# A squared-ReLU feed-forward in two phases, its second product made of seven block products in place of eight

## The chip, the cores and the metric

The kernel runs on one core of a Trainium2 chip. Its time is the device time of one execution in microseconds (us), lower is better; the median of several runs counts. The engines named below are TensorE (PE, matrix products), VectorE (DVE), ScalarE (ACT), GpSimd (POOL) and SyncE (SP, which here only issues transfers between DRAM and the on-chip memory).

## The reference

One layer of a conditioned decoder trunk on x of 2048 tokens by 1024 channels, in float32. The part that the change touches is the squared-ReLU feed-forward; the token mixer before it (attention, convolutions, pooling and the output projection `w_out`) stays, but its last stage for the second half of the tokens borders on it.

```python
x = x + g1 * mix                                   # mix = concatenate([...]) @ w_out[l]
h = rms_norm(x, norm2_g[l]) * (1.0 + sc2) + sh2
x = x + g2 * (jnp.square(jax.nn.relu(h @ w_ff1[l])) @ w_ff2[l])
# w_ff1: 1024 x 4096, w_ff2: 4096 x 1024
```

## The kernel before

Tokens are worked on in two halves (`hc` = 0, 1) of 1024. For each half the output projection runs first (`out_part`, 8 rows of 128 tokens, each with two column blocks of 512), then the feed-forward. Between them x is normalised and turned into `h_hi` and `h_lo`.

A float32 product is made of three products of rounded operands. Each operand is split into a high part (ScalarE copies it into the type float32r: a "head") and the rest (VectorE subtracts: a "tail"), and TensorE adds hi x hi, hi x lo and lo x hi. Every matmul of the feed-forward has 128 stationary columns and 512 moving ones.

The hidden width of 4096 is cut into 16 groups `g` of 256. Per group:

- The first product gives u = relu(w1ᵀ h)² for 256 hidden rows and 1024 tokens. The two first groups (`plain`) do it directly with 96 matmuls. The other 14 (`fast`) use seven block products in place of eight (Winograd's form), 84 matmuls; they need three combinations of h made once per half (`comb_add`, `comb_tail`, `difference_tail`, `last_comb_sum`) and four sums of the group's weights (`w1_sum1` to `w1_sum4`), and their seven results go through PSUM banks 0 to 3 with copies by ScalarE (`seeded`, `copied`, `reseeded`).
- The second product (`second`) follows at once, direct: 16 output tiles (8 token tiles, two column blocks of 512) of 6 matmuls each, 96 a group, in PSUM banks 4 to 7. VectorE adds each tile to `x_new`, the half's x in on-chip memory (`accumulate`). The gate g2 has been multiplied into the weights of w_ff2 (`w2_fold`), then they are split.

Each engine has its own order, written out by hand, and semaphores tie them together. SyncE issues all loads, each when its buffer comes free. Groups 3 to 15 run in hardware loops (`Fori`). Rows of the result are stored from `x_new` as the last group's tiles are added.

## Time and profile before

| | |
|---|---|
| median of 3 runs | 2357.76 us (2356.51 to 2361.86) |
| span of the profiled execution, first to last instruction | 2354.6 us |
| TensorE busy | 2283.8 us, 97% |
| VectorE busy | 1746.0 us, 74% |
| ScalarE busy | 971.2 us, 41% |
| DMA, mean over the span | 75 GB/s |

The profile comes from one execution. Its span begins with the first and ends with the last instruction. What that execution took around its span is not recorded; the three timed runs lie 1.9 to 7.3 us above the span. Matmuls overlap, so the duration of one (389 ns) is longer than the distance from one start to the next; the second is what a stage costs. VectorE's short operations overlap a little too.

### The profile page before, as it was taken

What the parts mean: (1) busy time and instruction counts of PE and PEld (TensorE: products, weight loads), DVE (VectorE), ACT (ScalarE), POOL (GpSimd) and SP (SyncE); (2) the same over time, 40 slices, a digit from 0 to 9 for tenths busy, and PEclk for the clock granted to TensorE, in tenths of its full rate; (3) what the DMA queues carried; (4) which work ended last, traced back from release to release, by engine and by line L of the source; (5) the groups of instructions that cost most, each with busy time, mean ns of one, the idle gap of its engine ahead of it and who ended that gap; (6) DMA issues with size and microseconds to landing.
All of it is one profiled execution on the core that took longest, in us unless ns stands there. A gap on an engine that the chain in (4) does not pass through costs nothing.

```text
span 2354.6 us, 31383 instructions
## 1 busy us (share of the span) xinstructions
PE 2283.8 (97%) x11642; PEld 1924.3 (82%) x11642; DVE 1746.0 (74%) x2659; ACT 971.2 (41%) x1595; POOL 357.9 (15%) x285
## 2 busy tenths in 40 slices
PE   6999999988999999999999999999999999999999
PEld 5987898767889888888888888888888888888887
DVE  6648886889989876876767767676787676767676
ACT  4531555458888844332323232233432323222231
POOL 0442044824356610000000000000000000000000
PEclk9999999989999999999999999999999999999999
DMA  7441533120000152011111111145111111111112
GB/s 270 155 152 63 157 129 118 63 89 28 15 10 24 52 155 81 18 54 54 53 53 53 37 61 45 54 132 189 63 36 53 54 36 62 45 53 53 53 53 89
DMA packets 108280, 177.68 MB, mean 75 GB/s; under 512 B 5512, under 2 KB 77468, under 8 KB 107164
## 3 DMA queue, kind: packets, MB, share of 16 engines
q1 hardware_dynamic: 108100, 176.41, 22.6%
q8 instruction: 58, 0.95, 0.2%
q14 instruction: 34, 0.28, 0.0%
q10 hardware_dynamic: 88, 0.04, 0.0%
HBM read 152.84 MB, written 23.59 MB: 75 GB/s over the span
## 4 chain that ended last, share of the span: by engine, by line
PE 81%; DVE 10%; DMA 3%; issue 2%; ACT 2%; POOL 2%; SPq 0%; ACTq 0%; DVEq 0%; POOLq 0%
PE ps L2513 10%; PE ps L2512 10%; PE ps L2511 10%; PE ps L2550 8%; PE ps L2548 8%; PE ps L2549 8%; PE ps L2210 5%; PE ps L2212 5%; PE ps L2211 5%; PE ps L2401 3%; DVE ps L1615 2%; PE ps L2458 2%; PE ps L2456 2%; PE ps L2457 2%; DMA sb_w_raw<-in_w_in 2%
## 5 line engine op out<-in xcount | busy, mean ns | idle before, releaser
L1997 DVE TENSOR_TENSOR sb_x_new<-sb_x_new,ps 128x512 f32<-128x512 f32 x512 | 347.2, 684 | 107.5 <-PE ps L2513 102.0
L2511 PE MATMUL ps<-sb_w_hi,sb_u_hi 128*128 128x512 f32 x1024 | 398.3, 389 | 0.0
L2512 PE MATMUL ps<-sb_w_lo,sb_u_hi 128*128 128x512 f32 x1024 | 398.3, 389 | 0.0
L2513 PE MATMUL ps<-sb_w_hi,sb_u_lo 128*128 128x512 f32 x1024 | 398.3, 389 | 0.0
L2512 PEld LDWEIGHTS ps<-sb_w_lo,sb_u_hi 128*128 128x128 f32 x1024 | 192.2, 188 | 39.9
L2511 PEld LDWEIGHTS ps<-sb_w_hi,sb_u_hi 128*128 128x128 f32 x1024 | 192.2, 188 | 39.9
L2513 PEld LDWEIGHTS ps<-sb_w_hi,sb_u_lo 128*128 128x128 f32 x1024 | 192.2, 188 | 39.9
L2212 PE MATMUL ps<-sb_h_hi,sb_w_lo 128*128 128x512 f32 x512 | 199.4, 389 | 0.0
L1428 ACT ACTIVATE ps<-ps 128x512 f32<-128x512 f32 x28 | 16.3, 582 | 410.8 <-PE ps L2550 410.8
L2210 PE MATMUL ps<-sb_h_hi,sb_w_hi 128*128 128x512 f32 x448 | 177.5, 396 | 0.7 <-DVE sb_w_lo L1958 0.7
L2211 PE MATMUL ps<-sb_h_lo,sb_w_hi 128*128 128x512 f32 x448 | 174.4, 389 | 0.0
L2548 PE MATMUL ps<-sb_h_hi,sb_ring_hi 128*128 128x512 f32 x448 | 174.3, 389 | 0.0
L2549 PE MATMUL ps<-sb_h_lo,sb_ring_hi 128*128 128x512 f32 x448 | 174.3, 389 | 0.0
L1354 ACT ACTIVATE sb_u_hi<-sb_u_full 128x512 fp32r<-128x512 f32 x128 | 81.0, 632 | 192.0 <-DVE sb_u_full L1986 114.2
L1837 DVE TENSOR_SCALAR_CACHE_REDUCE sb_scores<-ps 128x1024 f32<-128x1024 f32 (+7 forms) x160 | 139.5, 891 | 12.4 <-PE ps L2424 6.9
L2401 PE MATMUL ps<-sb_v_sb,sb_a_t 128*128 128x64 f32 x1088 | 140.7, 270 | 0.0
L1615 DVE SCALAR_TENSOR_TENSOR ps<-sb_conf,sb_col,ps 128x512 f32<-128x512 f32 x208 | 140.4, 747 | 0.0
L2401 PEld LDWEIGHTS ps<-sb_v_sb,sb_a_t 128*128 128x128 f32 x1088 | 136.4, 195 | 0.5 <-ACT sb_q_stack L1258 0.2
L2421 PE MATMUL ps<-sb_k_stack,sb_q_stack 128*128 128x512 f32 (+3 forms) x320 | 112.8, 417 | 23.2 <-DVE sb_scores L1837 18.3
L2550 PE MATMUL ps<-sb_h_hi,sb_w_lo 128*128 128x512 f32 x336 | 130.7, 389 | 0.0
L2548 PE MATMUL ps<-sb_w_hi,sb_ring_hi 128*128 128x512 f32 x336 | 130.7, 389 | 0.0
L2549 PE MATMUL ps<-sb_w_lo,sb_ring_hi 128*128 128x512 f32 x336 | 130.7, 389 | 0.0
(291 smaller groups left out, 4947.9 us busy)
## 6 DMA issues: line engine op xcount, KB each, us to landing
sb_w_full<-in_w_ff SPq DMA_DIRECT2D x34, 1024.0 KB, 4.9
sb_w_full<-in_w_ff SPq DMA_DIRECT2D x56, 512.0 KB, 3.7
sb_w_raw<-in_w_in SPq DMA_DIRECT2D x16, 1024.0 KB, 5.6
sb_ada<-in_w_ada SPq DMA_DIRECT2D x32, 512.0 KB, 5.0
sb_ada_first<-in_w_ada SPq DMA_DIRECT2D x8, 1024.0 KB, 13.7
sb_x_in<-in_x SPq DMA_DIRECT2D x16, 512.0 KB, 5.4
sb_mix_in<-mix_scratch SPq DMA_DIRECT2D x16, 512.0 KB, 4.9
sb_x_new<-in_x SPq DMA_DIRECT2D x16, 512.0 KB, 4.9
```

The lines of the kernel that those rows point to most:

```text
L1615: ins = V.scalar_tensor_tensor(out=dst, in0=src, scalar=w, in1=dst, op0=ALU.mult, op1=ALU.add)
L1997: V.tensor_tensor(out=y, in0=y, in1=psum[:, 4 + p % 4, :], op=ALU.add).then_inc(ff2_read, 1)
L2210: M(dst, ah, bh, start=(n == 0), stop=False)
L2211: M(dst, ah, bl, start=False, stop=False)
L2212: ins = M(dst, al, bh, start=False, stop=(n == last))
L2401: ins = M(psum[:, 6 + i % 2, hd * VD:(hd + 1) * VD], a_t[gn % 3][:, k * P:(k + 1) * P], v_sb[:, k0 + k, hd * VD:(hd + 1) * VD], start=(k0 ...
L2511: M(dst, uh, wh[:, j, col], start=j == order[0], stop=False, skip_group_check=fast)
L2512: M(dst, uh, wl[:, j, col], start=False, stop=False, skip_group_check=fast)
L2513: ins = M(dst, ul, wh[:, j, col], start=False, stop=j == order[1], skip_group_check=fast)
L2548: M(psum[:, bank, :], wh[:, k, :], rh[:, k, :], start=fresh and k == 0, stop=False, skip_group_check=True)
L2549: M(psum[:, bank, :], wh[:, k, :], rl[:, k, :], start=False, stop=False, skip_group_check=True)
L2550: ins = M(psum[:, bank, :], wl[:, k, :], rh[:, k, :], start=False, stop=k == DC // 2 - 1, skip_group_check=True)
```

## The change

The feed-forward of a half is split into two phases.

- Phase one makes the first products of all 16 groups and no second product. Each u (four blocks: two of hidden rows by two of tokens) is not split, but stored to DRAM in the seven forms that the second phase needs: three blocks of u as they are and four sums (`u_sums`, `u_sum4`), 256 KB each, into `left_scratch`.
- Phase two works through 8 chunks `c` of 512 hidden rows. Each chunk is a product of 1024 tokens x 512 by 512 x 1024, made of seven block products ("slots") of 512 x 256 by 256 x 512 in place of eight. SyncE loads the seven left blocks (512 KB each) and the right side (2 MB of w_ff2); VectorE makes four sums of the right side (`right_add`); both sides of each slot are split (`heads`, `left_tail`, `right_tail`). All eight PSUM banks hold results: side 0 is banks 0 to 3, side 1 is banks 4 to 7. ScalarE copies between the sides (`seed_lower`, `seed_upper`), and VectorE reads five partial results per chunk, each in two pieces of two banks, into sums in on-chip memory (`evacuate`).
- Since x no longer fits beside these, it goes to DRAM after the output projection (`x_mid_scratch`) and comes back in the last chunk. There the gate g2 is multiplied onto the results, by GpSimd for the upper rows (`finish_upper`) and VectorE for the lower, and x is added.
- The weights of phase one are double-buffered by group, with one 1 MB load each; the loops are written out.
- The two plain groups now follow each other directly, and the output projection of the second half follows the last chunk of the first.

The core of the diff, cut ("..." marks what is left out). TensorE:

```diff
-                def second(g, p, js, fast):
-                    t, cb = tile_no(p, fast)
-                    wh, wl = by_k2(w_hi[3][:, :]), by_k2(w_lo[3][:, :])
...
                 def plain(g):
...
                         if f >= 2:
                             pe.wait_ge(relu_ready, 4 * (PLAIN * hc + g) + f - 1)
+                        elif g and f == 0:
+                            pe.wait_ge(relu_ready, 4 * (PLAIN * hc + g))
...
                 def fast(g):
                     n = FAST * hc - PLAIN + g
-                    fast_product(n, 0, 0, True, rows(0, 0))
-                    if g is PLAIN:
-                        pe.wait_ge(t_lo, 4 * hc + 3)
-                    fast_product(n, 1, 2, True, combined(0)[0:2])
+                    if g == PLAIN:
+                        pe.wait_ge(relu_ready, 4 * PLAIN * (hc + 1))
+                    else:
+                        pe.wait_ge(fast_relu, 2 * n - 1)
+                    fast_product(g, 0, 0, True, slot(0)[0:2])
...
+                def multiply(G, s, t, side, fresh):
+
+                    hi, low, _ = slot(s)
+                    dst, tok = psum[:, 4 * side + t, :], slice(t * P, (t + 1) * P)
+                    for k in range(2):
+                        M(dst, hi[:, k, tok], hi[:, 2 + k, :], start=fresh and k == 0, stop=False, skip_group_check=True)
+                        M(dst, hi[:, k, tok], low[:, 2 + k, :], start=False, stop=False, skip_group_check=True)
+                        ins = M(dst, low[:, k, tok], hi[:, 2 + k, :], start=False, stop=k == 1, skip_group_check=True)
+                    ins.then_inc(part_mm, 1)
+
+                def chunk(c):
+                    G, last = chunk_no(hc, c), c == CHUNKS - 1
+                    for s in order_of(c):
+                        pe.wait_ge(slot_lo, 2 * (SLOTS * G + s) + 2)
+                        for t in range(4):
+                            if s == 0 and c:
+                                pe.wait_ge(part_read, read_no(hc, c - 1, 5, t // 2))
...
+                            elif s == 1:
+                                pe.wait_ge(part_copied, copy_no(G, 0, t))
+                            elif s == 3:
+                                pe.wait_ge(part_copied, copy_no(G, 1, t))
+                            elif s == 5:
+                                pe.wait_ge(part_read, read_no(hc, c, 1 if last else 3, t // 2))
+                            elif s == 6:
+                                pe.wait_ge(part_read, read_no(hc, c, 4, t // 2))
+                            multiply(G, s, t, 1 if s in (2, 4, 6) else 0, s in (0, 5))
```

`order_of(c)` is 0 to 6, and 0, 1, 5, 2, 3, 4, 6 in the last chunk of a half. ScalarE, the end of the plain groups and phase two:

```diff
+                relu(1, 1)
+                w1_head(PLAIN, 0)
+                w1_head(PLAIN, 1)
+                w1_head(PLAIN, 2)
+                relu(1, 2)
+                w1_head(PLAIN, 3)
+                w1_head(PLAIN, 4)
+                w1_head(PLAIN, 5)
+                w1_head(PLAIN, 6)
+                relu(1, 3)
+                last_comb_head()
...
+                def seed_upper(c):
+                    G = chunk_no(hc, c)
+                    for t in range(4):
+                        act.wait_ge(part_mm, part_no(G, order_of(c).index(2), t))
+                        act.wait_ge(part_read, read_no(hc, c, 5 if c == CHUNKS - 1 else 1, t // 2))
+                        A(psum[:, t, :], psum[:, 4 + t, :], ACT.Copy).then_inc(part_copied, 1)
+
+                for c in range(CHUNKS - 1):
+                    heads(c, 5)
+                    seed_lower(c)
+                    heads(c, 6)
+                    heads(c + 1, 0)
+                    seed_upper(c)
+                    for s in range(1, 5):
+                        heads(c + 1, s)
```

VectorE, the second plain group, a fast group, and phase two:

```diff
-                def accumulate(g, p, fast=False):
-                    t, cb = tile_no(p, fast)
-                    y = x_new[:, t, cb * BLK:(cb + 1) * BLK]
-                    dve.wait_ge(ff2_mm, 16 * g + (16 * FG * hc + p + 1))
-                    V.tensor_tensor(out=y, in0=y, in1=psum[:, 4 + p % 4, :], op=ALU.add).then_inc(ff2_read, 1)
...
+                link(comb_add(t1, b22[0], t2, ALU.subtract))
+                comb_add(t1, t1, b22[1], ALU.add).then_inc(t_summed, 1)
+                u_sums(0)
+                u_sum4(0)
+                difference_tail()
+                last_comb_sum()
+                plain_square(1, 0)
+                comb_tail(1, 2)
+                plain_square(1, 1)
+                comb_tail(0, 3)
+                w1_sums(PLAIN)
+                for i in range(3):
+                    w1_tail(PLAIN, i)
+                plain_square(1, 2)
...
+                        dve.wait_ge(fast_relu, 2 * n)
+                        square(1, 0)
+                        u_sum4(g - 1)
+                    if last:
+                        right_add(0, 0)
+                        right_add(0, 1)
+                    else:
+                        w1_sums(g + 1)
+                        for i in range(3):
+                            w1_tail(g + 1, i)
                     dve.wait_ge(fast_relu, 2 * n + 1)
                     square(0, 0)
-                    dve.wait_ge(fast_mm, 7 * n + 5)
+                    if last:
+                        tails(0, 0)
...
+                for c in range(CHUNKS - 1):
+                    if c:
+                        evacuate(c - 1, 6, 1)
+                        tails(c, 5)
+                    else:
+                        tails(0, 2)
+                        dve.wait_ge(fast_relu, 2 * (fast_no(FG - 1) + 1))
+                        square(1, 0)
+                        u_sum4(FG - 1)
+                        tails(0, 3)
+                        tails(0, 4)
+                        tails(0, 5)
+                    tails(c, 6)
+                    right_add(c + 1, 0)
+                    evacuate(c, 1, 0)
+                    evacuate(c, 1, 1)
...
+                if hc == 0:
+                    wo_tail(1, 1)
+                    mix_tail(HT)
+                    mix_tail(HT + 1)
+                for t in range(4):
+                    dve.wait_ge(part_mm, part_no(chunk_no(hc, c), SLOTS - 1, t))
+                    ins = V.tensor_tensor(out=out21[:, t, :], in0=psum[:, 4 + t, :], in1=gate_row[:, 1, 0:BLK], op=ALU.mult)
```

SyncE, a fast group and phase two:

```diff
+                        fast_done(hc, g - 1, SLOTS)
+                    if g < FG - 1:
+                        load_w1(hc, g + 1)
+                    else:
+                        load_right(0)
+                    store_left_sums(hc, g - 1)
+                    if g > PLAIN:
+                        store_left_u(hc, g - 1, 5, 4)
+                    store_left_sum4(hc, g - 1)
...
+                for ch in range(CHUNKS - 1):
+                    G = chunk_no(hc, ch)
+                    if ch == 0:
+                        sp.wait_ge(slot_lo, 2 * SLOTS * G + 8)
+                        sp.wait_ge(right_summed, 4 * G + 4)
+                        load_right(1)
+                    for s in range(SLOTS):
+                        if s == 6 and ch + 2 < CHUNKS:
+                            sp.wait_ge(slot_lo, 2 * SLOTS * (G + 1) + 8)
+                            sp.wait_ge(right_summed, 4 * (G + 1) + 4)
+                            load_right(ch + 2)
+                        sp.wait_ge(part_mm, part_no(G, s, 3))
+                        load_left(hc, ch + 1, s)
```

## Rows read from the trace of the kernel before

**Rows 1.** The page, its first part: busy time and share of the span by engine.

```profile
PE 2283.8 (97%) x11642; PEld 1924.3 (82%) x11642; DVE 1746.0 (74%) x2659; ACT 971.2 (41%) x1595; POOL 357.9 (15%) x285
```

**Rows 2.** Window: busy PE, PEld, DVE, ACT, POOL; clock, DMA share, GB/s.

```profile
1000.00:1650.00 650.00, 650.00 (x2885) 538.58 (x2884) 457.08 (x625) 188.49 (x287) 0.00 (x0) 1.00 0.22 71
```

**Rows 3.** Waits: who waited for whom, us in total, times, longest.

```profile
ACT ps L1428 <- PE ps L2550: 410.8, 28, 15.2
...
DVE sb_x_new L1997 <- PE ps L2513: 102.0, 154, 0.7
```

**Rows 4.** Timeline, PE, border of the halves: start, us, engine, line.

```profile
1556.26 0.39 PE L2548 MATMUL ps<-sb_h_hi,sb_ring_hi 128*128 128x512 f32 x1
...
1575.30 0.39 PE L2511 MATMUL ps<-sb_w_hi,sb_u_hi 128*128 128x512 f32 x1
...
1597.06 0.39 PE L2456 MATMUL ps<-sb_w_hi,sb_h_hi 128*128 128x512 f32 x1
```

**Rows 5.** Groups by form, from 1000 us: busy us, mean ns, idle before.

```profile
L1997 DVE TENSOR_TENSOR sb_x_new<-sb_x_new,ps 128x512 f32<-128x512 f32 x496 | 337.1, 684 | 107.4 <-PE ps L2513 102.0
...
L1380 ACT ACTIVATE sb_ring_hi<-sb_w_full 128x512 fp32r<-128x512 f32 x112 | 69.7, 622 | 1.3
...
L1434 ACT ACTIVATE ps<-ps 128x512 f32<-128x512 f32 x28 | 16.3, 582 | 44.9 <-PE ps L2550 44.9
...
L1284 ACT ACTIVATE sb_h_hi<-sb_mix_in 128x1024 fp32r<-128x1024 f32 x8 | 8.4, 1047 | 0.2 <-DMA sb_mix_in<-mix_scratch 0.2
```

**Rows 6.** Timeline, DVE: operations of 512, then of 1024 and 2048 columns.

```profile
1544.47 0.68 DVE L1997 TENSOR_TENSOR sb_x_new<-sb_x_new,ps 128x512 f32<-128x512 f32 x1
1545.07 0.68 DVE L2026 TENSOR_TENSOR sb_w_lo<-sb_w_full,sb_ring_hi 128x512 fp32r<-128x512 f32 x1
...
1594.45 1.22 DVE L1873 TENSOR_TENSOR sb_h_lo<-sb_mix_in,sb_h_hi 128x1024 fp32r<-128x1024 f32 x1
1595.59 1.28 DVE L1997 TENSOR_TENSOR sb_x_new<-sb_x_new,ps 128x512 f32<-128x512 f32 x2
...
1599.27 2.29 DVE L1894 TENSOR_TENSOR sb_w_lo<-sb_wo_raw,sb_w_hi 128x2048 fp32r<-128x2048 f32 x1
```

**Rows 7.** DMA issues: count, KB each, median us from issue to landing.

```profile
sb_w_full<-in_w_ff SPq DMA_DIRECT2D x34, 1024.0 KB, 4.9
sb_w_full<-in_w_ff SPq DMA_DIRECT2D x56, 512.0 KB, 3.7
...
sb_ada_first<-in_w_ada SPq DMA_DIRECT2D x8, 1024.0 KB, 13.7
...
sb_v_sb<-qkv_scratch SPq DMA_DIRECT2D x1, 2048.0 KB, 10.0
```

**Rows 8.** Last tail of h, second half; TensorE's feed-forward began at 1691.0.

```profile
L2210 PE MATMUL ps<-sb_h_hi,sb_w_hi x32: 389/389/504, 1691.0 to 1713.6; 128*128 128x512 f32 x32
...
1701.88 1.23 DVE L1493 TENSOR_TENSOR sb_h_lo<-sb_h_tmp,sb_h_hi 128x1024 fp32r<-128x1024 f32 x1 [0.40 <-ACT sb_h_hi L1018]
```

**Rows 9.** Groups of POOL: its commonest operation of 1024 columns.

```profile
L908 POOL TENSOR_TENSOR sb_gate_row<-sb_gate_row,sb_ada 128x1024 f32<-128x1024 f32 x21 | 52.9, 2532 | 55.7 <-ACT sb_ada L1139 55.7
```

**Rows 10.** Timeline of the end; the span is 2354.6 us.

```profile
2350.49 0.39 PE L2513 MATMUL ps<-sb_w_hi,sb_u_lo 128*128 128x512 f32 x1
2350.91 0.69 DVE L1997 TENSOR_TENSOR sb_x_new<-sb_x_new,ps 128x512 f32<-128x512 f32 x1 [0.67 <-PE ps L2513]
```

**Rows 11.** Timeline of PE around a gap in the attention stage.

```profile
824.48 0.61 PE L2386 MATMUL ps<-sb_ident,sb_scores 128*128 128x128 f32 x4
...
825.76 0.61 PE L2386 MATMUL ps<-sb_ident,sb_scores 128*128 128x128 f32 x4
...
830.68 1.11 PE L2386 MATMUL ps<-sb_ident,sb_scores 128*128 128x128 f32 x4 [2.02 <-ACT sb_a_t L1258]
...
833.19 1.06 PE L2386 MATMUL ps<-sb_ident,sb_scores 128*128 128x128 f32 x4
```

**Rows 12.** Window behind that gap: the columns are those of rows 2.

```profile
831.00:833.00 2.00, 2.00 (x12) 2.00 (x11) 2.00 (x2) 0.72 (x2) 0.82 (x1) 0.50 1.06 402
```

More of the change, by code:

```diff
@@ L837, in _ @@
+                for e in range(HT):
+                    store_out(hc, e)
+                    if hc == 0 and e == HT // 2 - 1:
+                        load_rows(1, 0)
+                        load_rows(1, 1)
+            for p in range(HT // 2):
+                sp.wait_ge(out_st[p], 64)
         @block.gpsimd
@@ new lines, in fast @@
+                    if last:
+                        heads(0, 1)
+                        heads(0, 2)
+                        heads(0, 3)
+                    else:
+                        for i in range(3, SLOTS):
+                            w1_head(g + 1, i)
+                    act.wait_ge(fast_mm, SLOTS * n + 7)
+                    last_square_free(g)
+                    A(u_full[1][0][:, :], psum[:, 1, :], ACT.Relu).then_inc(fast_relu, 1)
+                for g in range(PLAIN, FG):
+                    fast(g)
@@ L1453, in _ @@
+                heads(CHUNKS - 1, 5)
+                seed_lower(CHUNKS - 1)
+                heads(CHUNKS - 1, 6)
+                seed_upper(CHUNKS - 1)
                 if hc == 0:
-                    for i in range(3):
-                        wo_head(1, i)
+                    G = chunk_no(0, CHUNKS - 1)
+                    wo_head(1, 0, (part_mm, part_no(G, 1, 3)))
+                    wo_head(1, 1, (part_mm, part_no(G, 3, 3)))
+                    act.wait_ge(part_mm, part_no(G, 4, 3))
@@ L2155, in fast @@
                     square_of_positive(1, 1)
-                    u_tail(g, 1, 0, 0)
-                    u_tail(g, 2, 1, 1)
-                    dve.wait_ge(fast_mm, 7 * n + 6)
+                    if last:
+                        right_add(0, 2)
+                        right_add(0, 3)
+                    else:
+                        for i in range(5, SLOTS):
+                            w1_tail(g + 1, i)
+                    dve.wait_ge(fast_mm, SLOTS * n + 6)
                     V.tensor_tensor(out=u_full[0][1][:, :], in0=psum[:, 3, :], in1=u_part[:, :],
@@ L2189, in _ @@
-                with dve.Fori(PLAIN + 1, FG - 1) as g:
-                    fast(g)
-                fast(FG - 1, last=True)
-                for p in range(4, 16):
-                    if hc == 0 and p in (6, 8, 10):
-                        wo_tail(1, p // 2 - 3)
-                    if hc == 0 and p in (12, 14):
-                        mix_tail(HT + p // 2 - 6)
-                    accumulate(FG - 1, p, True)
-                if hc == 0:
+                    if last:
+                        tails(0, 1)
@@ L2587, in _ @@
                 for g in range(PLAIN):
                     plain(g)
-                fast(PLAIN)
-                with pe.Fori(PLAIN + 1, FG) as g:
+                for g in range(PLAIN, FG):
                     fast(g)
+                for c in range(CHUNKS):
+                    chunk(c)
 INPUTS = ["x", "c", "w_ada", "b_ada", "norm1_g", "norm2_g", "w_in", "w_out", "q_norm_g", "k_norm_g",
```

878 lines of the change are left out of this document (506 added, 372 removed).

## The prediction, written before the changed kernel was run

> **What bounds the kernel now.** I read the totals of the page first, then the windows, the waits and the timelines of the feed-forward. TensorE is busy for 97% of the span and VectorE for 74% [rows 1]. The windows say where the rest lies: from 1000 to 1650 us, over the border of the halves, TensorE is busy for all 650 us at full granted clock [rows 2]. The chain of waits agrees: VectorE and ScalarE wait there for TensorE, not TensorE for them [rows 3]. A busy TensorE is not yet TensorE at its pace, so I take the pace from the timeline: a group's first product starts at 1556.26, its second at 1575.30 and the next stage at 1597.06 [rows 4]. That is 84 matmuls in 19.04 us and 96 in 21.76 us, both 0.2267 us each, without a gap over the border of a half. So the feed-forward costs its number of matmuls times 0.2267 us; a matmul that goes away is worth that, as long as nothing else falls due first.
>
> **What is removed.** Before, the second product of a half is 16 groups of 96 matmuls, 1536. Now it is 8 chunks of 7 block products of 4 token tiles, 2 hidden blocks and 3 part products: 8 x 7 x 24 = 1344. Over two halves 384 go: 384 x 0.2267 = **87.0 us**. The first product keeps its matmuls, and the shape (128 columns stationary, 512 moving) stays.
>
> **Phase one, one fast group (84 matmuls, 19.04 us).** VectorE loses its 16 accumulations, the fold of the gate and the splits of u; it keeps 4 weight sums, 7 weight tails, 4 squares, 2 sums, and gains 4 sums of u: 21 operations of 512 columns. Each is listed at about 0.69 us [rows 5], but ready ones follow each other after 0.60 us [rows 6]: 12.6 us by pace, 14.5 us by duration. ScalarE has 5 reads of PSUM and 7 heads of 0.62 us, 7.3 us [rows 5]. The order matters more. The next group's weights (1 MB, one issue) are only asked for when the previous group ends, and land 4.9 us later [rows 7]; with issue at about 5.3 us. From there VectorE runs 4 sums (7.8), 3 tails (10.6), a square after the fourth product (12.1), 2 tails (13.3), the sum that frees bank 1 (14.3), a square, 2 tails, the second sum (17.0), a square and 3 sums of u (19.7), while its next work, the last square, falls due at 19.8. TensorE needs bank 1 for its seventh product at 16.3, so 2 us are spare. I cost the 28 groups at nothing; the cover is that spare time. The seven stores of 256 KB per group and the load are 2.8 MB; two rows that differ by 512 KB differ by 1.2 us [rows 7], so about 7 us of transfer in 19. The removed loops give nothing back, since the groups already follow without a gap [rows 4].
>
> **Phase two, one chunk (168 matmuls, 38.08 us).** VectorE has 14 tails, 4 sums of the right side and 10 evacuations, all of 1024 columns. No row shows an evacuation of two banks at once; at 512 columns a read from PSUM costs the same 0.684 us as one from SBUF [rows 5], so 1.15 us by pace [rows 6], 1.22 by duration: 28 x 1.15 = 32.2 us, at most 34.2. ScalarE: 14 x 1.05 + 8 x 0.58 = 19.3 us. Both are under 38.08. In the program's order the tightest date is the copy of side 1 to side 0 before the fourth product (16.3 us into the chunk): it needs the evacuation of the second product (due 8.2, done 9.4) and a ScalarE that has got past the heads for the next chunk's slot 0. The 2 MB of the right side are asked for some 5 us before the chunk starts. The nearest rows are 4.9 us for 1 MB plus 2.5 for a second one, 7.4, and 10.0 for a 2 MB load [rows 7]; so they are there at 3 to 5 us, and the date holds with over 5 us spare. Steady chunks: nothing.
>
> **The plain stage of each half.** The second products of the two plain groups, 43.5 us of cover, are no longer between the first ones. TensorE needs 2 x 21.76 us, but VectorE must in that time form and split the combinations of h and prepare seven weights. Counted from TensorE's start, its last tail of h ends at 12.1 [rows 8]. Following the program at 0.6, 1.15 and 2.2 us for 512, 1024 and 2048 columns (2.29 listed [rows 6], less the overlap): first pass over the combinations 14.4, square 15.0, second pass 17.2, tail of the second weights 19.4, two squares, a wait for the fourth relu, 23.8 (TensorE waits too, 0.8 us, since the second plain group now needs all four), square, two passes 28.9, four sums of u 31.6, tail 33.9, fourth combination 38.7, two squares and two tails 44.3, first weight sum 44.9, fourth 46.9. ScalarE has three heads behind those sums ahead of the last relu, and four more: that relu ends at 49.7. TensorE would be done at 45.6 and its next product waits for that relu: 4.1 us. Together 5.0 us a half, **10.0 us** (0 to 20: three microseconds of VectorE either way count in full).
>
> **From phase one to two.** In the last group the 2 MB load comes first and the u stores behind it. I put the right side at 9 us (7.4 to 12), the first left block at 11. ScalarE does the heads of slot 0 ahead of the relu of bank 0, so that ends at 13.6; VectorE's square and two tails follow, and the sum that frees bank 1 ends at 17.2 against 16.3: 0.9 us. TensorE enters chunk 0 at 20.0. VectorE is behind: tails of slot 2 at 28.4, of slot 3 at 32.0, only then may the next 2 MB be asked for, landing at 40. VectorE's sum of that right side stands *before* the evacuation of the second product. So the evacuation due at 31 ends at 42.4, the copy at 43.6, and TensorE, which was ready at 36.3, starts its fourth product at 43.7: 7.4 us. Per half 8.3 us, **16.7 us** (6 to 28).
>
> **Between the halves.** Before, there is no gap [rows 4]. Now the output projection waits until VectorE has read the last block's first two tiles, and that stands behind scaling, adding, a weight tail of 2.2 us and two mix tails: read at 43.7 of the last chunk, which TensorE leaves at 38.5. Then the weight tails of parts 2 and 3 cost 0.6, and the last product began 0.4 late: **6.3 us** (3 to 12). GpSimd's finish of the upper rows, 2.5 us each of eight steps [rows 9], lies beside this.
>
> **The end.** Today the last matmul starts at 2350.49, VectorE ends at 2351.6, the span at 2354.6 [rows 10]: 3.7 us after the last matmul. Afterwards VectorE owes two scalings and two additions more and is a little behind: about 7.1 us, so **3.4 us**.
>
> **The clock.** After a gap of 2.02 us a round of 12 small matmuls takes 2.5 us in place of 1.3 [rows 11], and the granted clock is 0.50, which is 1.2 GHz [rows 12]; two such rounds cost 2.4 us. The three gaps above 6 us would each bring this: **7.2 us** (0 to 12; the two of 4 us might as well). The Trainium skill (TensorE: Matmul & The Clock Gate, Why this matters for your kernels) says that TensorE sent waiting between bursts of matmuls falls back to half its clock; this case's trace agrees, with its 0.50. By that rule the change loses at five places; without any such loss the sum would give 2307.
>
> **Sum.** -87.0 + 10.0 + 16.7 + 6.3 + 3.4 + 7.2 = -43.4. The profiled span of 2354.6 becomes 2311.2. The runs lie 3.2 us above the span (median 2357.76), so 2314.4; I say **2314 us**.
>
> **Rivals.**
> A (0.12): the borders are covered after all. For it: VectorE's dates there hang on landings that I put late. Half of my stalls and no clock loss leave 18 us: 2289.
> B (0.20): phase one is paced by VectorE behind the weight load. For it: 2 us are all that is spare, and with other traffic a 1 MB load took up to 13.7 us [rows 7]. Against: here it stands ahead of the stores. If it lands at 8.5 us, each group loses 1.2 us, 28 groups 34: 2348.
> C (0.05), the other side: the same load lands above 9 us. From 7.3 us on every microsecond is paid 28 times; the remaining 43 us of gain are gone at 1.5 us per group, so from 8.8 us on the kernel is slower; at 9.5 it is 2.2 us per group, 62 us: 2376.
> D (0.05): a chunk is paced by VectorE. At 1.4 us an operation a chunk takes 39.2, 16 x 1.1 = 18 us: 2332. The widest 1024-column row, 1.22, speaks against it.
> The forecast has the remaining 0.58.
>
> **How the numbers follow.** The forecast's own range, from the bounds above, is 2295 to 2335. The 80% range reaches halfway into A and into the mild end of B: 2292 to 2345. No change means within 0.2%, 4.7 us, which a measurement of this kernel can just tell. Slower is C, 0.05; same, between B and C, 0.03; faster 0.92.
>
> **What the profile afterwards would show.** 1344 matmuls a half in the second product, at 0.2267 us; fast groups 19.04 us apart and chunks 38.1; gaps of TensorE of about 4 us before the first fast group, 7 before chunk 0's fourth product, 5 between the halves, each followed by a granted clock of 0.50. I am wrong if fast groups are over 19.3 us apart (B, C), chunks over 38.3 (D), or the borders are closed (A).

## The result, and the profile after

The changed kernel takes 2344.09 us (median of 4 runs, 2341.91 to 2347.80), the kernel before 2359.64 us on the same chip: a ratio of 0.9937 (95% interval 0.9922 to 0.9951), 15.6 us faster. A second comparison of the same pair on another occasion gave 2343.36 against 2356.66 us, 0.9950 (0.9937 to 0.9964). So the change is worth some 13 to 16 us; the forecast was a gain of 43, and 2344 us lies at the very end of the range (2292 to 2345) and outside the forecast's own (2295 to 2335). The direction was right, two thirds of the gain are missing.

The page of the changed kernel, its head and first part:

```profile
span 2346.0 us, 29756 instructions
...
PE 2230.1 (95%) x11258; PEld 1875.4 (80%) x11258; DVE 1840.0 (78%) x2575; ACT 1121.7 (48%) x1787; POOL 404.3 (17%) x301
```

TensorE has exactly 384 matmuls fewer than in [rows 1], and VectorE is busy for 94 us more. The profiled execution is the slowest of the four (2347.8 us), and the profiled one of before, with its span of 2354.6, was the fastest of its four (2356.51). So the two spans differ by 8.6 us only, where the medians differ by 15.6. I account for these 8.6.

Windows of the changed kernel, columns as in [rows 2]: up to the feed-forward, its first half, the output projection of the second half, the second feed-forward, and a stretch inside the first half (each row ends with the granted clock, the share of the transfers and GB/s):

```profile
0.00:943.60 943.60, 881.48 (x5378) 765.83 (x5378) 738.32 (x1315) 555.18 (x965) 358.06 (x285) 0.97 0.30 100
943.60:1596.30 652.70, 626.16 (x2721) 514.88 (x2721) 520.40 (x583) 269.91 (x378) 23.78 (x8) 0.98 0.46 159
1596.30:1692.50 96.20, 95.86 (x440) 79.38 (x440) 64.75 (x96) 35.87 (x76) 0.00 (x0) 0.98 0.39 131
1692.50:2338.40 645.90, 626.16 (x2719) 515.31 (x2720) 512.82 (x579) 260.75 (x372) 22.50 (x8) 0.98 0.45 153
1000.00:1250.00 250.00, 250.00 (x1105) 207.07 (x1104) 176.60 (x275) 87.97 (x157) 0.00 (x0) 1.00 0.47 155
```

From 1000 to 1250 us TensorE is busy throughout at full granted clock, as before: the fast groups run as forecast. But each half of the feed-forward has about 20 to 26 us in which TensorE does nothing, and the mean clock of a half is 0.98 in place of 1.00. The timeline of TensorE shows where; these are the first matmuls behind its waits (start, duration, line, and in brackets the idle time and who ended it):

```profile
993.37 0.75 PE L2844 MATMUL ps<-sb_h_hi,sb_w_hi 128*128 128x512 f32 x1 [3.49 <-ACT sb_u_full L1590]
...
1264.71 0.79 PE L2844 MATMUL ps<-sb_h_hi,sb_w_hi 128*128 128x512 f32 x1 [5.62 <-DVE sb_u_full L2375]
1265.30 0.63 PE L2845 MATMUL ps<-sb_h_lo,sb_w_hi 128*128 128x512 f32 x1
1265.73 0.63 PE L2846 MATMUL ps<-sb_h_hi,sb_w_lo 128*128 128x512 f32 x1
...
1291.00 0.77 PE L2878 MATMUL ps<-sb_h_hi 128*128 128x512 f32 x1 [4.52 <-ACT ps L1677]
...
1579.18 0.47 PE L2878 MATMUL ps<-sb_h_hi 128*128 128x512 f32 x1 [3.63 <-DVE sb_out L2343]
...
1587.94 0.80 PE L2878 MATMUL ps<-sb_h_hi 128*128 128x512 f32 x1 [4.44 <-DVE sb_out L2343]
...
1596.29 0.76 PE L2772 MATMUL ps<-sb_w_hi,sb_h_hi 128*128 128x512 f32 x1 [4.02 <-DVE sb_out L2508]
...
2333.63 0.79 PE L2878 MATMUL ps<-sb_h_hi 128*128 128x512 f32 x1 [4.89 <-DVE sb_out L2343]
```

The first half has six such gaps, the second four, of 3.6, 5.1, 5.6 and, in its last chunk, 5.1 us. Behind each of them the matmuls start 0.43 us apart (1265.30 to 1265.73), not 0.2267; the window 1264.70 to 1269.50 has a granted clock of 0.50. From gaps (start to start, less 0.23) and from the slow matmuls (their distance less 0.2267) comes the ledger, in us of the profiled span:

| term | forecast | measured, half 0 + half 1 |
|---|---|---|
| 384 matmuls | -87.0 | -87.0 (pace 0.2267) |
| plain stage | +10.0 | +9.2 (4.6 + 4.6) |
| phase one to two, chunk 0 | +16.7 | +21.2 (10.5 + 10.7) |
| last chunk, and between the halves | +6.3 | +17.9 (12.8 + 5.1) |
| end (last matmul to the end of the span) | +3.4 | +3.5 |
| clock behind the gaps | +7.2 | +19.6 (10.4 + 9.2) |
| before the feed-forward starts | 0 | +6.3 |
| sum | -43.4 | -9.3 (span: -8.6) |

The row "before the feed-forward starts" is not the change: the instructions there are the same. The feed-forward starts at 937.29 us in the trace of before and at 943.61 in this one, and in the twelve traces of experiments below, whose work up to there is the same too, anywhere from 936.25 to 943.60, with a median of 940.1. It differs by stretches of low clock in the attention stage: from 700 to 800 and from 800 to 900 us the granted clock is 0.97 and 0.93 in the first trace of the changed kernel, and 1.00 in both in the run that starts at 936.25. One trace of before, of its fastest execution, can't say whether a shift of one to three microseconds is left in the mean.

### The profile page after: what moved, and what is told of

Read it like the earlier page. It is cut to its first block and busy times, and to the rows that moved or that the text cites. A ratio compares the mean times of both kernels' runs of the same rounds, so it can differ in the third digit from the quotient of the medians.

```text
span 2346.0 us, 29756 instructions
## 1 busy us (share of the span) xinstructions
PE 2230.1 (95%) x11258; PEld 1875.4 (80%) x11258; DVE 1840.0 (78%) x2575; ACT 1121.7 (48%) x1787; POOL 404.3 (17%) x301
## 5 line engine op out<-in xcount | busy, mean ns | idle before, releaser
L2878 PE MATMUL ps<-sb_h_hi 128*128 128x512 f32 x512 | 203.6, 398 | 23.1 <-DVE sb_out L2343 13.0
L2879 PE MATMUL ps<-sb_h_lo,sb_h_hi 128*128 128x512 f32 x512 | 202.2, 395 | 0.0
L2880 PE MATMUL ps<-sb_h_hi,sb_h_lo 128*128 128x512 f32 x512 | 202.2, 395 | 0.0
L2844 PE MATMUL ps<-sb_h_hi,sb_w_hi 128*128 128x512 f32 x448 | 178.2, 398 | 17.6 <-DVE sb_u_full L2375 10.6
L2527 PE MATMUL ps<-sb_h_hi,sb_w_hi 128*128 128x512 f32 x448 | 177.8, 397 | 0.7 <-DVE sb_w_lo L2195 0.7
L2845 PE MATMUL ps<-sb_h_lo,sb_w_hi 128*128 128x512 f32 x448 | 177.5, 396 | 0.0
L2528 PE MATMUL ps<-sb_h_lo,sb_w_hi 128*128 128x512 f32 x448 | 174.4, 389 | 0.0
L2076 DVE TENSOR_SCALAR_CACHE_REDUCE sb_scores<-ps 128x1024 f32<-128x1024 f32 (+7 forms) x160 | 139.6, 891 | 15.6 <-PE ps L2741 8.5
L2879 PE MATMUL ps<-sb_w_lo,sb_w_hi 128*128 128x512 f32 x384 | 149.4, 389 | 0.0
L2878 PE MATMUL ps<-sb_w_hi 128*128 128x512 f32 x384 | 149.4, 389 | 0.0
L2880 PE MATMUL ps<-sb_w_hi,sb_w_lo 128*128 128x512 f32 x384 | 149.4, 389 | 0.0
L2343 DVE TENSOR_TENSOR sb_out<-sb_out,ps 128x1024 f32<-128x1024 f32 x108 | 130.0, 1215 | 9.5 <-PE ps L2880 9.5
L2844 PE MATMUL ps<-sb_w_hi,sb_w_hi 128*128 128x512 f32 x336 | 130.8, 389 | 0.0
```

Source lines behind the costliest of these rows:

```text
L2076: V.tensor_scalar(prob(u, m, c0, n), sc_pair(r)[:, 0:n], -SCALE, None, ALU.mult, ALU.min, accum_out=part_min[:, s, m, c0 // WIDE:c0 // WID ...
L2527: M(dst, ah, bh, start=(n == 0), stop=False)
L2528: M(dst, ah, bl, start=False, stop=False)
L2844: M(psum[:, bank, :], wh[:, k, :], rh[:, k, :], start=fresh and k == 0, stop=False, skip_group_check=True)
L2845: M(psum[:, bank, :], wh[:, k, :], rl[:, k, :], start=False, stop=False, skip_group_check=True)
L2878: M(dst, hi[:, k, tok], hi[:, 2 + k, :], start=fresh and k == 0, stop=False, skip_group_check=True)
```

## The experiments

Each run was timed in five rounds with the kernel before on the same chip. "Won" is the median of before less that of the run, in the same comparison. Four rows share a comparison with the changed kernel: its second timing and the three below it, in which GpSimd's finish is cut, chunk 0 is reordered and the last fast group is reordered. The others were timed on other chips, where the median of before lay 1.4 us higher (2358.04 and 2358.12; 2356.67 for the last row), so their distance to the changed kernel is uncertain by a microsecond or two.

| run | median us | ratio to before (95%) | won, us |
|---|---|---|---|
| changed kernel, first / again | 2344.09 / 2343.36 | 0.9937 / 0.9950 (0.9937 to 0.9964) | 15.6 / 13.3 |
| GpSimd's finish cut | 2327.37 | 0.9871 (0.9856 to 0.9886) | 29.3 |
| chunk 0 reordered | 2335.59 | 0.9913 (0.9900 to 0.9927) | 21.1 |
| last fast group reordered | 2334.81 | 0.9911 (0.9898 to 0.9925) | 21.9 |
| plain stage reordered | 2342.16 | 0.9940 (0.9926 to 0.9954) | 15.9 |
| PE kept busy in the gap | 2340.62 | 0.9923 (0.9910 to 0.9935) | 17.4 |
| last chunk reordered | 2339.41 | 0.9920 (0.9907 to 0.9933) | 18.6 |
| all four orders | 2319.23 | 0.9833 (0.9820 to 0.9845) | 38.8 |
| three orders, without the last chunk's | 2320.26 | 0.9836 (0.9823 to 0.9850) | 37.9 |
| finish on VectorE | 2344.34 | 0.9944 (0.9930 to 0.9957) | 13.8 |
| left block loaded earlier | 2332.56 | 0.9894 (0.9879 to 0.9910) | 25.6 |
| all four orders and the load | 2319.25 | 0.9844 (0.9828 to 0.9860) | 37.4 |

**The changed kernel again.**

> The changed kernel as it is, for comparison on the same chip. If the later start of the feed-forward (943.6 us against 937.3) belongs to single executions, this trace shows another start than 943.6, with other stretches of low clock in the attention stage; if it belongs to the change, it starts at 943 to 944 again. Ratio to the kernel before about 0.994.

Ratio 0.9950. Its feed-forward starts at 939.78, with the same instructions and the same gaps at its borders (3.7, 5.7, 5.6, 3.9, 3.7, 3.9 us in half 0): the late start belongs to single executions, the gaps to the kernel.

**The last chunk: GpSimd beside VectorE.** What holds TensorE there is VectorE. Timelines of VectorE and of GpSimd in the changed kernel's second trace, the last chunk of half 0:

```profile
1571.10 3.59 DVE L2133 TENSOR_TENSOR sb_w_lo<-sb_w_full,sb_w_hi 128x2048 fp32r<-128x2048 f32 x1
1574.61 1.21 DVE L2343 TENSOR_TENSOR sb_out<-sb_out,ps 128x1024 f32<-128x1024 f32 x1
1575.85 2.14 DVE L2470 TENSOR_TENSOR sb_out<-sb_out,sb_gate_row 128x1024 f32<-128x1024 f32 x1
1578.03 5.51 DVE L2475 TENSOR_TENSOR sb_x_pair<-sb_x_pair,sb_out 128x512 f32<-128x512 f32 x2
1583.46 1.21 DVE L2343 TENSOR_TENSOR sb_out<-sb_out,ps 128x1024 f32<-128x1024 f32 x1
1584.70 1.22 DVE L2470 TENSOR_TENSOR sb_out<-sb_out,sb_gate_row 128x1024 f32<-128x1024 f32 x1
1585.96 1.29 DVE L2475 TENSOR_TENSOR sb_x_one<-sb_x_one,sb_out 128x512 f32<-128x512 f32 x2
```

```profile
1570.13 2.41 POOL L1166 TENSOR_TENSOR sb_out<-sb_out,sb_gate_row 128x1024 f32<-128x1024 f32 x1 [8.36 <-DVE sb_out L2343]
1572.62 4.29 POOL L1169 TENSOR_TENSOR sb_x_pair<-sb_x_pair,sb_out 128x1024 f32<-128x1024 f32 x1
1576.86 3.38 POOL L1166 TENSOR_TENSOR sb_out<-sb_out,sb_gate_row 128x1024 f32<-128x1024 f32 x1
1580.31 2.68 POOL L1169 TENSOR_TENSOR sb_x_pair<-sb_x_pair,sb_out 128x1024 f32<-128x1024 f32 x1
```

The same two additions of 512 columns take 5.51 us while GpSimd works and 1.29 behind it. The read of PSUM at 1574.61 falls in the middle of GpSimd's 4.29 us and takes its usual 1.21. And GpSimd's own four operations range from 2.41 to 4.29 us. The times fit turns: the second of VectorE's two additions ends half a microsecond after GpSimd's last operation (1583.54 and 1582.99). So the theory: operations of VectorE with both operands in on-chip memory and GpSimd's exclude each other. Two runs test it. In the first, GpSimd works on 8 columns of each block only (the upper rows of the result then lack most of the feed-forward):

```diff
-link(pool.tensor_tensor(out=y, in0=y, in1=gate_row[:, 1:2, col].to_broadcast([P, 2, BLK]), op=ALU.mult))
+link(pool.tensor_tensor(out=y[:, :, 0:8], in0=y[:, :, 0:8], in1=gate_row[:, 1:2, a * BLK:a * BLK + 8].to_broadcast([P, 2, 8]), op=ALU.mult))
```

with the addition cut in the same way.

> GpSimd's work in the last chunk is cut from 512 to 8 columns of each block (the upper rows of the result then lack most of the feed-forward). Theory, GpSimd's additions slow VectorE: VectorE's 128x1024 operations between buffers in the last chunk go from 3.3 to 1.2 us, its two additions from 5.5 to 1.3, and PE's gaps there (3.9 of 4.0 us between halves, 3.6 and 4.4 in the last chunk of half 0, 4.9 in that of half 1) shrink to under 1 us each with their stretches of low clock: 12 to 20 us faster than the changed kernel. Rival, VectorE's operations are slowed by the transfers that run at the same time: durations and gaps stay, and the time stays within 2 us.

16.0 us less than the changed kernel in the same comparison. VectorE's timeline at the same place:

```profile
1568.44 2.29 DVE L2133 TENSOR_TENSOR sb_w_lo<-sb_w_full,sb_w_hi 128x2048 fp32r<-128x2048 f32 x1
1570.64 1.21 DVE L2343 TENSOR_TENSOR sb_out<-sb_out,ps 128x1024 f32<-128x1024 f32 x1
1571.89 1.22 DVE L2470 TENSOR_TENSOR sb_out<-sb_out,sb_gate_row 128x1024 f32<-128x1024 f32 x1
1573.15 1.29 DVE L2475 TENSOR_TENSOR sb_x_pair<-sb_x_pair,sb_out 128x512 f32<-128x512 f32 x2
```

The gaps in both last chunks are gone; the one between the halves stays and is 5.5 us, against the 5.2 of waiting (43.7 less 38.5) that the forecast had worked out without GpSimd. So GpSimd's finish, which the forecast put "beside", cost 16 us. In the second run VectorE does the eight operations of each half itself and GpSimd none:

```diff
+def finish_upper(s, a):
...
+    for p in range(2):
+        scaled(sum_of(s, p), a, 2)
+    for p in range(2):
...
+        rows = x_pair[p][:, :, a * BLK:(a + 1) * BLK]
+        V.tensor_tensor(out=rows, in0=rows, in1=sum_of(s, p), op=ALU.add).then_inc(upper_done, 1)
...
+finish_upper(1, 0)
 evacuate(c, 3, 0)
...
+finish_upper(3, 1)
```

> VectorE takes over GpSimd's eight operations of the last chunk (upper rows by the gate, and into the rows); GpSimd does nothing there. Theory, two operands in on-chip memory are served to one of the two engines at a time: VectorE's slowed operations go back to 1.22 us and its two additions to 1.3, it gains 10 us of duration and pays 8 x 1.15 = 9 us for the new work, so its queue ends within 2 us of where it did and the kernel's time stays within 3 us of the changed kernel's. Rival, the slow operations come from the transfers into the rows that run then: VectorE's operations stay at 3.3 and 5.5 us, its queue is 9 us longer in each half, and the kernel 12 to 18 us slower than the changed one.

Groups of VectorE in that run, 1548 to 1600 us (count, busy us, mean ns):

```profile
L2467 DVE TENSOR_TENSOR sb_out<-sb_out,sb_gate_row 128x1024 f32<-128x1024 f32 x8 | 9.8, 1222 | 0.2
...
L2130 DVE TENSOR_TENSOR sb_w_lo<-sb_w_full,sb_w_hi 128x2048 fp32r<-128x2048 f32 x3 | 6.8, 2283 | 0.0
L2481 DVE TENSOR_TENSOR sb_x_pair<-sb_x_pair,sb_out 128x1024 f32<-128x1024 f32 x4 | 4.7, 1220 | 0.1
L2472 DVE TENSOR_TENSOR sb_x_pair<-sb_x_pair,sb_out 128x512 f32<-128x512 f32 x6 | 3.9, 688 | 0.1
```

Everything is back to 1.22 and 0.69 us, and the program issues the same transfers, so it is not the transfers. And the time is that of the changed kernel (2344.34 against 2343.36 and 2344.09). TensorE still waits for VectorE at the end of half 0, 3.0 and 9.6 us in place of 3.9, 3.7 and 3.9. In half 1 VectorE takes as long in both from its read of the last chunk's second product to its end: from 2299.53 to 2339.57 with GpSimd's help, from 2296.45 to 2336.42 without it, 40.0 us each. Sharing this work with GpSimd is worth nothing here.

The Trainium skill has the rule (SBUF — State Buffer, Who interferes with whom): "A DVE instruction with two SBUF inputs contends with a GpSimd instruction that reads SBUF", as an exclusive lock. These traces agree: 5.51 against 1.29 us for two inputs in on-chip memory, 1.21 us either way with one in PSUM. The forecast did not weigh this rule.

**The last chunk: is it the order?** The reads of PSUM are not slowed, so they can go first. In half 0 the additions into the rows stand last:

```diff
 evacuate(c, 3, 0)
 evacuate(c, 3, 1)
+evacuate(c, 4, 0)
+evacuate(c, 4, 1)
 if hc == 0:
     wo_tail(1, 0)
+    wo_tail(1, 1)
+    mix_tail(HT)
+    mix_tail(HT + 1)
 for p in range(2):
-    evacuate(c, 4, p)
     scaled(sum_of(4, p), 1, 2)
-    for t in (2 * p, 2 * p + 1):
-        add_to_row(4 + t, 1, out22[:, t, :])
...
```

(The additions follow further down, in half 0 behind all of the last product's reads.)

> In the last chunk GpSimd keeps its work. VectorE's four reads of the fifth product's banks stand directly behind those of the fourth, and in half 0 all additions into the rows stand behind the last product's reads. Theory, reads of PSUM keep their 1.21 us beside GpSimd, and the gaps come from the slowed operations that stand ahead of them: the gaps of 3.7 and 3.5 us in half 0 and of 5.0 us in half 1 go, that at the end of half 0 (3.9 us) stays within 2 us of that, and the time is 10 to 16 us below the changed kernel's, nearly that of the run with GpSimd's work cut. Rival, VectorE simply has too much to do in the last chunk: the waits are taken over by the gap at the end of half 0 and by the end of the kernel, and no more than 5 us are won.

The theory of order was half right. The reads of PSUM keep their pace beside GpSimd (four in 4.72 us in half 0) and the gaps inside the last chunk go, but in half 0 one gap takes their place, and in half 1 TensorE's last matmul starts at 2325.21 while VectorE works on to 2336.4. The timeline of TensorE at the end of half 0:

```profile
1578.93 0.39 PE L2890 MATMUL ps<-sb_h_hi,sb_h_lo 128*128 128x512 f32 x1
1591.01 0.76 PE L2782 MATMUL ps<-sb_w_hi,sb_h_hi 128*128 128x512 f32 x1 [11.69 <-DVE sb_out L2516]
```

11.9 us in one place against 11.6 in three (second trace of the changed kernel). Some 4 us were won: fewer gaps mean fewer stretches of low clock, and in half 1 one gap of 5.0 us is gone, but the kernel's end then waits for VectorE. The rival holds: in the last chunk VectorE is the bound, and an order only moves the wait.

**From phase one to two.** The first block of the second weights' left side is a transfer that ScalarE copies ahead of the nonlinearity of bank 0. ScalarE's timeline in the last fast group of half 0, which began at 1238.8, in the second trace of the changed kernel:

```profile
1247.16 0.58 ACT L1638 ACTIVATE ps<-ps 128x512 f32<-128x512 f32 x1 [2.12 <-PE ps L2846]
1254.72 1.06 ACT L1618 ACTIVATE sb_h_hi<-sb_h_lo_full 128x1024 fp32r<-128x1024 f32 x1 [6.98 <-DMA sb_h_lo_full<-left_scratch]
1255.69 1.04 ACT L1623 ACTIVATE sb_h_hi<-sb_right 128x1024 fp32r<-128x1024 f32 x1
1256.63 0.58 ACT L1646 ACTIVATE sb_u_full<-ps 128x512 f32<-128x512 f32 x1
```

The block lands 15.9 us after the group's start; the forecast had 11 (its 9 us for the right side holds: VectorE starts on that at 1247.78). One run takes the nonlinearity past the wait:

```diff
-if last:
-    heads(0, 0)
-else:
+if not last:
     w1_head(g + 1, 1)
     w1_head(g + 1, 2)
...
 A(u_full[0][0][:, :], psum[:, 0, :], ACT.Relu).then_inc(fast_relu, 1)
 if last:
+    heads(0, 0)
     heads(0, 1)
```

(ScalarE; on VectorE `tails(0, 0)` moves in the same way.)

> In the last fast group, ScalarE applies the nonlinearity to bank 0 before it copies the first block of the second weights, and VectorE takes that copy's difference after the second sum of activations. Theory, the gap at the border of the phases (5.8 us in half 0, 5.1 in half 1) comes from ScalarE waiting for a transfer (the left block landed 15.9 us after the group began) ahead of the nonlinearity: both gaps shrink to under 2 us, 8 to 12 us faster than the changed kernel with the clock. Rival, the copy's difference then comes late for the second phase: the gap moves by some hundred columns of matmuls and keeps its length.

8.6 us less. The border's gap falls from 5.7 to 2.3 and 1.5 us in half 0 and from 5.0 to 2.3 in half 1. The waits of 2.3 us are now for VectorE's difference of that same block, the 1.5 for ScalarE's last nonlinearity of the group, which comes behind the moved copies. The other run leaves the queues of the engines and issues the load ahead of five stores of 256 KB (the expectation counts four):

```diff
 load_right(0)
+fast_done(hc, g, 1)
+load_left(hc, 0, 0)
 store_left_sums(hc, g - 1)
...
-        for s in range(3):
+        for s in range(1, 3):
```

> In the last fast group the load of the first left block stands ahead of four of the stores of activations (sums of the group before). Theory, the block landed 15.9 us after the group's start because the load was issued behind these stores and shared the engines with them: it lands 11 to 13 us after the start, and the gap at the border of the phases (5.8 and 5.1 us) falls to 1 to 3 us, 5 to 10 us faster than the changed kernel. Rival, it is the 2 MB of right-hand weights ahead of it that hold it: it lands 14 us or later, and the gap falls by less than 2 us.

ScalarE's timeline of that run, whose last group began at 1236.7:

```profile
1245.07 0.58 ACT L1640 ACTIVATE ps<-ps 128x512 f32<-128x512 f32 x1 [2.12 <-PE ps L2848]
1247.10 1.06 ACT L1620 ACTIVATE sb_h_hi<-sb_h_lo_full 128x1024 fp32r<-128x1024 f32 x1 [1.45 <-DMA sb_h_lo_full<-left_scratch]
...
1249.02 0.58 ACT L1648 ACTIVATE sb_u_full<-ps 128x512 f32<-128x512 f32 x1
```

It lands after 10.4 us, the gap is 1.8 us in half 0 and 1.5 in half 1, and some 11 us are won over the changed kernel, for one load that is issued past five stores. SyncE's timelines say which part of this is the issue and which the way (the second trace of the changed kernel, then this run):

```profile
1242.59 0.52 SPq L870 DMA_DIRECT2D sb_h_lo_full<-left_scratch  x1
```

```profile
1239.62 0.53 SPq L870 DMA_DIRECT2D sb_h_lo_full<-left_scratch  x1
```

Counted from the group's start the load is issued 0.9 us earlier (2.9 in place of 3.8) and takes 7.5 us to land in place of 12.1. So it was the stores' transfers ahead of it that held it, not SyncE. The 2 MB of the right side are ahead of it in both; they are not what made it 15.9 us.

**Chunk 0.**

```diff
-right_add(c + 1, 0)
+if c:
+    right_add(c + 1, 0)
 evacuate(c, 1, 0)
 evacuate(c, 1, 1)
+if c == 0:
+    right_add(c + 1, 0)
```

(VectorE; on ScalarE `heads(c + 1, 0)` moves behind `seed_upper(c)` in chunk 0.)

> In chunk 0 alone, the second eviction of the seventh product stands before the addition that waits for the next weights, and ScalarE's seed before the copy of those weights. Theory, the gap ahead of chunk 0's fourth product (4.7 us in half 0, 5.6 in half 1) is this order: both gaps fall to under 1.5 us, and their low-clock stretches (1.2 and 2.1 us) with them: 10 to 13 us faster than the changed kernel, unless the late weights reappear as a gap ahead of chunk 1. Rival, the weights themselves are late for chunk 1 as well: the gap moves behind and the time stays within 3 us.

7.8 us less: the gaps fall from 5.6 and 5.7 to 2.6 and 2.4 us, not to under 1.5, and no gap appears ahead of chunk 1. The rest is VectorE's delay from the border before it: with the last fast group reordered as well, these gaps are 0.7 and 0.6 us (three orders together, below).

**The plain stage, and the clock.** The forecast had ScalarE's last nonlinearity behind seven weight copies.

```diff
 w1_head(PLAIN, 0)
-w1_head(PLAIN, 1)
-w1_head(PLAIN, 2)
 relu(1, 2)
-w1_head(PLAIN, 3)
-w1_head(PLAIN, 4)
-w1_head(PLAIN, 5)
-w1_head(PLAIN, 6)
+w1_head(PLAIN, 1)
 relu(1, 3)
+for i in range(2, SLOTS):
+    w1_head(PLAIN, i)
```

(On VectorE `w1_sums(PLAIN)` and the first `w1_tail` move ahead of `comb_tail(0, 3)`.)

> At the end of the plain group, ScalarE applies the last two nonlinearities before it copies blocks 1 to 6 of the first fast group's weights, and VectorE takes their differences of sums before the last difference of halves. Theory, the gap ahead of the first fast group (3.65 us of engine time in each half) is the nonlinearity behind the copies: it falls under 1.5 us in both halves, with its low-clock stretch (1.7 and 2.7 us): 6 to 9 us faster than the changed kernel. Rival, the weight copies are then late: the gap moves by a few hundred matmul columns and stays as long, the time within 2 us.

Some 1 to 2 us won, within the measurement. The gap of 3.65 us falls to 0.85, and 11 us later TensorE waits 2.9 us in half 0 and 2.4 in half 1 for ScalarE, which is now late with its reads of PSUM. The rival was right in the main: the wait moved, though further than it had said, and most of its length stayed. The second run leaves the wait and gives TensorE work in it:

```diff
 if g == PLAIN:
+    for k in range(14):
+        M(psum[:, 0, :], h_hi[:, k % DC, 0:P], h_hi[:, k % DC, 0:BLK], start=True, stop=True, skip_group_check=True)
     pe.wait_ge(relu_ready, 4 * PLAIN * (hc + 1))
```

> Fourteen additional matmuls, whose result nothing reads, in the wait ahead of the first fast group: some 3.2 us of the 3.65 us wait is then filled with work, and what PE waits for is as it was. It prices the clock alone. Theory, the low-clock stretch behind a gap costs as much as the trace's pace says (1.7 and 2.7 us): the group starts at the same time and runs at 0.2267 us a matmul from its first, 3 to 5 us faster than the changed kernel. Rival, the slow pace behind the gap is something else (the restart of the pipeline, or the engines behind it): the stretch of 0.43 us a matmul stays and the time is the same.

Windows of the changed kernel's first trace behind that gap, and then of this run (the last figures: granted clock, share and rate of the transfers):

```profile
993.40:996.40 3.00, 3.00 (x7) 2.40 (x8) 3.00 (x6) 1.81 (x2) 0.00 (x0) 0.51 0.00 0
```

```profile
986.50:990.00 3.50, 3.21 (x15) 2.32 (x13) 3.50 (x7) 3.50 (x8) 0.00 (x0) 1.00 0.00 0
990.00:993.00 3.00, 2.96 (x13) 2.46 (x14) 3.00 (x6) 1.89 (x2) 0.00 (x0) 1.00 0.00 0
```

7 matmuls in 3 us at 1.2 GHz, 13 at 2.4 GHz, with the other engines doing the same: the slow pace behind a gap is the clock. From the last plain matmul to the border of the phases the trace has 2.5 us less over both halves than the changed kernel's second one, and 3 us are won in the median, at the edge of what comparisons on two chips can tell. The clock had taken 4.4 there; part came back as gaps of 0.6 and 0.4 us further on, where TensorE was early for ScalarE.

**Together.**

> The reorderings of chunk 0, of the last fast group, of the plain group's end and of the last chunk together. Theory, the borders are separate causes and add up: the sum of the single gains (7.8 and 8.6 us measured, 6 to 9 and 10 to 16 us expected) is 32 to 41 us, 2302 to 2311 us. Rival, part of each gain is taken back at the next border, since VectorE's and ScalarE's queues run through: 2315 to 2325 us.

> The reorderings of chunk 0, of the last fast group and of the plain group's end together, with the last chunk as in the changed kernel. The single runs gave 7.8, 8.6 and 1.2 us, all four together 24.1. Theory, the borders are separate: 17 to 19 us below the changed kernel, 2324 to 2327 us, and the order of the last chunk was worth the other 5 to 7. Rival, the borders feed one another: over 2331 us or under 2321 us.

> The four reorderings together (2319.2 us) and the earlier load of the first left block. Theory, what was left of the border of the phases (gaps of 2.3 and 1.5 us in half 0, 2.3 us in half 1, and 1.7 us of low clock) is the first block's copy and difference, which wait for that load: 3 to 6 us less, 2313 to 2316 us. Rival, with ScalarE's nonlinearity already ahead of the copy the load has no one left who waits for it: within 1 us of 2319.

Three orders without the last chunk's win 37.9 us over the kernel before, some 23 more than the changed kernel and more than the 7.8, 8.6 and 1 to 2 of the single runs. The rival was right: the border and chunk 0 are one chain of delay, and undoing one alone left part of the other's (2.6 and 2.4 us at chunk 0, against 0.7 and 0.6 now). All four orders land in their rival's range too, but not for its reason: the borders gave more together than alone, and it is the order of the last chunk that adds only 0.9 us, which can't be told from nothing. The long wait at the end of half 0 (12 us) is there in place of the three. The earlier load adds nothing either, as its rival said, once the nonlinearity no longer waits for it; the gap of 2.3 us that stays is for VectorE's difference, which the reordering itself had put late. All three still carry the last chunk's loss.

## Why the prediction was wrong

**Right:** the pace and the bound. 384 matmuls are gone at 0.2267 us, the fast groups and the chunks in between run without a gap, weights for a group arrive in time: rivals B, C and D are out, and A, since no border is covered. The places and, but for the last chunk, the causes of the waits were right too. The plain stage (10.0 against 9.2), the end (3.4 against 3.5), the length of the wait between the halves without GpSimd (5.5 in the run with its work cut).

**The step that failed most is the sentence "GpSimd's finish of the upper rows ... lies beside this".** It took GpSimd's price from [rows 9] and cost it to nobody. On the chip the two engines exclude each other. VectorE loses about 10 us in each last chunk; where its queue was the nearest to due, that became gaps of 3.8, 4.9 and 5.1 us with a stretch of low clock each. Measured: 16.0 us for both halves together, clock included. The forecast had no term and no bound for it. Since VectorE is the bound of the last chunk, the work is not free on either engine: done by VectorE alone it costs the same. The trace of before could have warned. An operation of VectorE on 128x1024, L1873, takes 1.22 us in [rows 6], where GpSimd does nothing; its group up to 937 us has a mean of 1.71 (groups by form of the kernel before, VectorE, 0 to 937 us):

```profile
L1873 DVE TENSOR_TENSOR sb_h_lo<-sb_mix_in,sb_h_hi 128x1024 fp32r<-128x1024 f32 x8 | 13.6, 1707 | 0.1
```

The timelines of VectorE and of GpSimd show why: six of the eight take 1.22 us with GpSimd idle, and these two take 6.23 together, just while it works.

```profile
826.67 6.23 DVE L1873 TENSOR_TENSOR sb_h_lo<-sb_mix_in,sb_h_hi 128x1024 fp32r<-128x1024 f32 x2
```

```profile
826.64 1.89 POOL L948 TENSOR_TENSOR sb_scores<-sb_scores,sb_ratio 128x1024 f32<-128x1024 f32 x1 [1.42 <-DVE sb_scores L1857]
828.61 3.21 POOL L949 TENSOR_TENSOR sb_scores<-sb_scores 128x1024 f32<-128x1024 f32 x1
```

**The clock was mis-sized: 7.2 forecast, 19.6 measured.** I let only the three gaps above 6 us count, at 2.4 us each. In the changed kernel all ten gaps, of 3.6 us and more, brought the low clock, 1.2 to 2.7 us apiece (one run with an edit has a gap of that length without it, see the last section). The remark in brackets, "the two of 4 us might as well", was the right reading of [rows 11], where 2.02 us had been enough, and it was not in the sum. The bound of 12 was too low as well, because the gaps in the last chunks were not foreseen.

**From phase one to two: 16.7 forecast, 21.2 measured, inside its bounds but with the parts exchanged.** The border itself cost 5.8 and 5.1, not 0.9: of the first left block I said 11 us, it was 15.9, since five stores stood ahead of it in the queue, and without them it takes about what I said (10.4). Chunk 0 cost 4.7 and 5.6, not 7.4.

**Most likely not the kernel's:** 6.3 us of the profiled trace are from before the feed-forward and vary from run to run. In the medians the miss is 28 us of gain (43.4 forecast, 15.6 measured): 16 of them GpSimd beside VectorE with its clock, some 5 the border, and the rest, by the ledger, the clock behind the other gaps. Against the forecast's 2314 it is 30, because the kernel before came out 1.9 us higher in this comparison (2359.64) than the 2357.76 it started from. That 2344 still lay inside the 80% range is luck: the range reached there for a late weight load (B), which did not happen.

**Open:** what the last chunk would cost with VectorE relieved by something other than GpSimd was not tried. That GpSimd's loss (4.29 in place of 2.4 us) is VectorE's hold on the same path was not tested by itself. Why one gap of 3.6 us is followed by the low clock and another isn't stays open too.

## What to carry to other kernels

When work is put on GpSimd to spare VectorE, look at what VectorE does in the same microseconds: two operands in on-chip memory on both sides, and the two run in turns; the sum of their work is then what counts, and only VectorE's reads of PSUM go on. When TensorE loses its cover at the borders of a loop, price every gap with its stretch of half clock (in the changed kernel 1.2 to 2.7 us for each of 3.6 us or more), and list per border the loads in the order of their queue, with the stores ahead of them: one load past five stores was worth some 11 us.

## What the runs showed of the hardware

- Two additions of 512 columns on VectorE take 5.51 us beside GpSimd's tensor-tensor operations and 1.29 without; an operation of 2048 columns 3.59 against 2.29; a read of PSUM 1.21 in both. GpSimd's operations of 1024 columns take 2.41 at their shortest and up to 4.29 beside VectorE.
- Shorter gaps too can bring the low clock, and don't always: at the border of the phases in the run with all four orders, a gap of 2.3 us was followed by 1.7 us of loss in half 1 and by none in half 0.
- A longer gap doesn't always bring it either. In the run with the finish on VectorE, the gap of 3.6 us ahead of half 1's first fast group was followed by full pace and a granted clock of 1.00, and the same gap in half 0 by 1.7 us of loss (timeline of TensorE, then the window behind it):

```profile
1739.90 0.50 PE L2852 MATMUL ps<-sb_h_hi,sb_w_hi 128*128 128x512 f32 x1 [3.49 <-ACT sb_u_full L1587]
1740.24 0.40 PE L2853 MATMUL ps<-sb_h_lo,sb_w_hi 128*128 128x512 f32 x1
```

```profile
1739.90:1741.00 1.10, 1.09 (x5) 0.92 (x6) 1.10 (x3) 1.10 (x1) 0.00 (x0) 1.00 0.00 0
```

- Two executions of the same instructions reach the feed-forward up to 7 us apart (936.25 and 943.60); from 800 to 900 us, in the attention stage, the granted clock was 1.00 in the first and 0.93 in the second.
